# Moving the cross-attention key projection of a fused decoder kernel to an earlier joint, with reciprocal square roots worked partly in PSUM

## The reference

```
x = x + gate * (retention(...) @ ret_w_out)          # first block, layer 0
h = rms_norm(x, norm_g[1]) * (1 + scale) + shift     # first block, layer 1: attention
...
mem_n = rms_norm(mem, norm_mem)                      # (256, 1024), gain norm_mem
x = x + concat(y_a, y_b, y_c) @ w_out                # mixer out
h = rms_norm(x, norm_cross)
q = rms_norm((h @ wq) per head, q_g)                 # 4 heads of 128
kv = mem_n @ wkv
k = rms_norm(kv[..., :512] per head, k_g)
v = kv[..., 512:]
x = x + softmax(q k^T / sqrt(128)) v @ wo
```

## Time and profile before

| what | us |
|---|---|
| device time, three runs | 1804.52, 1806.66, 1806.71 |
| median | 1806.66 |
| the profiled execution, its own time | 1805.74 |
| its span | 1803.9 |
| PE busy | 1763.1 (98%) |
| DVE, ACT, POOL busy | 931.5, 471.5, 1103.0 |
| granted clock of PE, mean | 0.99 |

### The profile page before, as it was taken

How to read it: one execution, slowest core, us unless ns; L and a number is a source line. 1 busy time by engine, 2 the same in 40 slices (tenths; PEclk the granted TensorE clock), 3 DMA queues, 4 the chain that set the end, 5 groups by cost and what they waited for, 6 DMA issues and landing times.

```text
span 1803.9 us, 26195 instructions
## 1 busy us (share of the span) xinstructions
PE 1763.1 (98%) x9198; PEld 1477.0 (82%) x9198; DVE 931.5 (52%) x1534; ACT 471.5 (26%) x958; POOL 1103.0 (61%) x848
## 2 busy tenths in 40 slices
PE   6999999999999999999999999989989999999998
PEld 4888888888888888888888778877878878888887
DVE  4754736574455545555443888786373463213311
ACT  4121221200233222322221247555332422002200
POOL 3656555698455444645457659864066588667863
PEclk9999999999999999999999999999999999999999
DMA  9523222385232222332223322200022333333331
GB/s 359 171 77 94 84 73 76 93 302 166 62 105 81 77 76 77 92 91 76 75 77 104 96 73 59 59 24 25 24 82 76 88 95 103 101 98 88 99 99 54
DMA packets 281588, 172.87 MB, mean 96 GB/s; under 512 B 6000, under 2 KB 272560, under 8 KB 280496
## 3 DMA queue, kind: packets, MB, share of 16 engines
q1 hardware_dynamic: 275024, 151.01, 28.5%
q10 hardware_dynamic: 6496, 20.93, 3.4%
HBM read 169.69 MB, written 2.10 MB: 95 GB/s over the span
## 4 chain that ended last, share of the span: by engine, by line
PE 92%; DVE 6%; SPq 1%; ACT 1%; DMA 0%; issue 0%; DVEq 0%; ACTq 0%
PE acc L390 14%; PE acc L392 14%; PE acc L391 14%; PE ob L390 4%; PE ob L392 4%; PE ob L391 4%; PE acc L420 3%; PE acc L422 3%; PE acc L421 3%; PE sc L1622 2%; PE acc L438 2%; PE acc L439 2%; PE acc L440 2%; PE sc L1543 1%; PE ob L1634 1%; PE acc L2035 1%
## 5 line engine op out<-in xcount | busy, mean ns | idle before, releaser
L766 POOL TENSOR_TENSOR wl<-raw,wh 128x512 fp32r<-128x512 f32 x456 | 638.6, 1421 | 19.3
L763 POOL TENSOR_SCALAR wh<-raw 128x1024 fp32r<-128x1024 f32 (+1 forms) x232 | 268.4, 1157 | 571.2 <-PE acc L392 143.5
L390 PE MATMUL acc<-hh,wh 128*128 128x512 f32 x800 | 325.6, 407 | 1.2 <-ACT sq L1413 1.2
L392 PE MATMUL acc<-hh,wl 128*128 128x512 f32 x800 | 313.7, 392 | 0.0
L391 PE MATMUL acc<-hl,wh 128*128 128x512 f32 x800 | 312.8, 391 | 0.0
L390 PEld LDWEIGHTS acc<-hh,wh 128*128 128x128 f32 x800 | 151.3, 189 | 35.5 <-issue 2.6
L391 PEld LDWEIGHTS acc<-hl,wh 128*128 128x128 f32 x800 | 151.5, 189 | 32.3 <-issue 2.4
L392 PEld LDWEIGHTS acc<-hh,wl 128*128 128x128 f32 x800 | 150.9, 189 | 33.0
L390 PE MATMUL ob<-Yh,wh 128*128 128x512 f32 x256 | 100.5, 393 | 0.0
L392 PE MATMUL ob<-Yh,wl 128*128 128x512 f32 x256 | 99.7, 390 | 0.0
L391 PE MATMUL ob<-Yl,wh 128*128 128x512 f32 x256 | 99.7, 389 | 0.0
(11 more groups left out here) (545 smaller groups left out, 3725.7 us busy)
## 6 DMA issues: line engine op xcount, KB each, us to landing
raw<-in_att_w_in SPq DMA_DIRECT2D x64, 512.0 KB, 4.0
raw<-in_mlp_w SPq DMA_DIRECT2D x64, 512.0 KB, 3.9
raw<-in_ret_w_in SPq DMA_DIRECT2D x48, 512.0 KB, 3.7
ada_w<-in_ada_w ACTq DMA_DIRECT2D x8, 1536.0 KB, 7.0
raw<-in_w_in SPq DMA_DIRECT2D x23, 512.0 KB, 3.6
ada_w<-in_ada_w SPq DMA_DIRECT2D x16, 512.0 KB, 8.9
raw<-in_ret_w_out SPq DMA_DIRECT2D x16, 512.0 KB, 4.3
raw<-in_att_w_out SPq DMA_DIRECT2D x16, 512.0 KB, 4.0
```

The source lines that it names most:

```text
L390: e.matmul(bank[:, :], wh[:, s, k, :], rhs_high(k), start=(start and k == 0), stop=False)
L392: last = e.matmul(bank[:, :], wl[:, s, k, :], rhs_high(k), start=False, stop=(stop and k == k1 - 1))
L763: e.tensor_scalar(wh[:, s, 0:k1, :], raw[:, s, 0:k1, :], 1.0, 1.0, ALU.mult, ALU.mult).then_inc(high_done, 1)
L766: low = e.tensor_tensor(wl[:, s, k0:k0 + KT // 2, :], raw[:, s, k0:k0 + KT // 2, :], wh[:, s, k0:k0 + KT // 2, :].bitcast(F32), ALU.subtract)
```

## The change

UNITS now has xa_k behind ret_out. The memory comes in a second time, transposed by the host (mem_t, 1 MB), so no PE transposes are left. It is loaded twice: into mem_t_early (where hh lies) during ret_out, for the keys, and into mem_t during the mixer's scan, for the values. At the first joint the keys are made without any root into the PSUM banks ob0 and ob1, evicted by ACT into xa_k_early, and written to a DRAM tensor, from which ACT's queue reads them back into xa_k in the second block, where their squares are taken in one ACT instruction and summed on PE behind mix_out unit 5. The token root (two columns) and the key roots (eight) are taken together, behind the mix_out loop. norm_roots and these roots run through roots_bank, which keeps copies in the bank st so that each step has at most one operand in SBUF. DVE's first attention sum waits for the keys' write, since the place is used again.

The diff, cut:

```diff
@@ norm_roots: rsqrt replaced @@
+        def roots_bank(e, a, n, name, work):
+            y, z = rs[:, 0, a:a + n], rs[:, 2, a:a + n]
+            yb, x, zb = (work[:, j, :] for j in range(3))      # in the bank st
+            def both(o, ob_, op):
+                op(ob_).then_inc(*V.done())
+                step(e, op(o), V)
+            both(y, yb, lambda o: e.tensor_scalar(o.bitcast(I32), x.bitcast(I32), -0.5, RSQRT_MAGIC, ALU.mult, ALU.add))
+            step(e, e.tensor_tensor(z, y, yb, ALU.mult), V)
...
         def norm_roots(e, tag, n=S):
             e.wait_ge(*PE.at(f"{tag}cols{KT - 1}"))
-            rsqrt(e, n // P, 1.0 / D, f"{tag}root")
+            w = root_work(n // P)
+            step(e, e.tensor_scalar(w[:, 1, :], st[:, 0:n // P], 1.0 / D, EPS, ALU.mult, ALU.add), V)
+            roots_bank(e, 0, n // P, f"{tag}root", w)
@@ ACT, retention out and first joint @@
             load_ada1(0)
             load_ada1(1)
+            e.dma_start(mte[:, :, :], mem_t).then_inc(mem_t_in, 16)
             ret_out_square(0)
             load_ada1(2)
             ret_out_square(1)
             load_ada1(3)
+            e.wait_ge(mem_t_in, 16)
             for n in range(2, KT):
                 if n % 2 == 0 and n + 3 < KT:
                     load_ada1(n + 2)
                     load_ada1(n + 3)
+                if n < 6:
+                    early_memory(2 * n - 4)
+                    early_memory(2 * n - 3)
+                if n == 6:
+                    early_high(0)
+                    early_high(1)
                 ret_out_square(n)
+            early_keys(0)
             norm_highs(e, "n1", lambda k: mod[:, 1, 0, k:k + 1])
+            early_keys(1)
+            e.wait_ge(*AC.at("x_ke1"))
+            e.dma_start(keys, xke[:, :, :].rearrange("p h n -> p (h n)")).then_inc(keys_out, 16)
@@ PE, first joint @@
+            early_keys(0)
             e.wait_ge(*V.at("mod1"))
             e.wait_ge(*V.at(f"ret_outss{KT - 2}"))
             columns(e, dg, 0, "first", False)
             e.wait_ge(*AC.at(f"ret_outsq{KT - 1}"))
             columns(e, sq[:, 1, :], 0, False, "last", f"n1cols{KT - 1}")
+            early_keys(1)
+            norm_spread(e, "n1")
+            early_keys(2)
             for n in range(16, 24):
                 last = e.matmul(sc[0][:, n:n + 1], ada_acc1[:, n * P:(n + 1) * P], ones[:, 0:1], start=True, stop=True)
             last.then_inc(*PE.done("ada1gate"))
-            norm_spread(e, "n1")
+            early_keys(3)
@@ DVE, retention out; first attention turn @@
                 ret_out_add(n)
+                if n == KT - 2:
+                    early_low(0)
                 ret_out_sum(n)
                 if n == KT - 2:
+                    early_low(1)
...
+            e.wait_ge(keys_out, 16)
             for n in range(4):
                 att_sum(0, "p", n)
@@ PE, second joint @@
-            def memory_steps(j):
-                if j < 2:
-                    memory_turned(2 * j + 4)
-                    memory_turned(2 * j + 5)
-            out_flat("mix_out", V.at(f"g_lo{GH - 1}"), KT, memory_steps)
-            for h in range(XH):          # the 4 xa_k units, with their column sums
...
+            def key_sums(j):
+                if j == 4:
+                    e.wait_ge(*AC.at("x_ksq"))
+                    for h in range(XH):
+                        columns(e, ksq[:, h, :], 16 + 2 * h, True, True, "x_kcols" if h == XH - 1 else None, n=2)
+            out_flat("mix_out", V.at(f"g_lo{GH - 1}"), KT, key_sums)
+            pair(e, U["xa_q"], U["xa_q"], "nx", [V.at(f"mix_outx{KT - 2 + b}") for b in range(2)])
@@ ACT, mix_out loop @@
-                if 1 <= j <= 2:
-                    memory_out(2 * j + 2)
-                    memory_out(2 * j + 3)
+                if 1 <= j <= 4:
+                    memory_out(2 * j - 2)
+                    memory_out(2 * j - 1)
+                if j == 3:
+                    e.wait_ge(keys_in, 16)
+                    e.activation(ksq[:, :, :], xk[:, :, :], ACT.Square).then_inc(*AC.done("x_ksq"))
                     memory_high(0)
@@ DVE, mix_out loop @@
                 mix_out_sum(j)
-                if j == 1:
-                    e.wait_ge(*AC.at("nkss1"))
-                    step(...); step(...)
-                    roots(e, 32, 2, "nkroot")
-                if j == 2:
-                    memory_low(0)
-                if j == 4:
-                    memory_low(1)
-            e.wait_ge(*PE.at("x_cols7"))
+            e.wait_ge(*PE.at("x_kcols"))
+            e.wait_ge(*AC.at("nkss1"))
+            w = root_work(10)
...
+            roots_bank(e, 16, 10, "xk_root", w)
+            memory_low(0)
+            memory_low(1)
```

125 lines of the change are left out of this document (66 added, 59 removed).

## The result

| | kernel before | changed kernel | ratio, 95% interval |
|---|---|---|---|
| first comparison, median | 1806.68 (1804.52 to 1807.44) | 1790.59 (1789.12 to 1792.87) | 0.9916 [0.9904, 0.9928] |
| again, on the chip of the last experiments | 1806.38 (1802.59 to 1808.66) | 1790.48 (1789.56 to 1792.47) | 0.9914 [0.9901, 0.9928] |
| the profiled execution, its own time | 1805.74 | 1789.37 | |
| its span | 1803.9 | 1787.6 | |
| mean granted clock of its span | 0.99 | 0.995 | |

The changed kernel is faster by 16 us in the medians. The forecast was 1795.6 with a range from 1793.0 to 1800.0, so the direction was right and the time came out 5.0 us under the forecast and 2.4 us under the range.

A forecast was written before the change was run, and what follows sets the result against it. PE, busy 98% of the span, was taken to bound the kernel. First joint 4.8 us more and second 15.9 less make 11.1 us less, so the median goes from 1806.66 to 1795.6, range 1793.0 to 1800.0.

The forecast's parts named there:

- First joint: From the last ret_out matmul to the attention's first pair issued: grows by 4.8 us, to 27.3, for 11.5 us of key work.
- one of the marks: Sign that the forecast is right: PE's granted clock is 1.00 between ret_out and the attention.
- The split of the 11.1 us into causes: Keys 1.2, mix_out's transposes and waits 4.3, first joint's clock about 2 and idle time 5, less 1.1 for new bubbles and waits.
- The root: Norm root in the first joint: twelve steps, none with two SBUF operands, 2.4 to 3.0 us; PE waits at most 0.2.
- hl beside POOL, and ACT's queue: First joint: each hl 1.42 us instead of 0.74 beside POOL; ACT's late query eviction costs up to 2.4, taken as 0.2.
- the first rival: First joint's cover incomplete: query eviction 2.4 us, roots 0.8, lower clock 2; time 1798.5 to 1801; chance 0.16.
- the second (clock): Clock stays at half through the whole first joint, key matmuls 8.9 us more: 1806.5, no change; chance 0.07.
- the third (memory late): Slow memory load delays the modulation's sums, PE waits ahead of the last ret_out unit; slower kernel; chance 0.03.
- Ahead of the first joint: Added ACT and DVE work and a 1 MB load before the joint lie in idle time: cost taken as nothing.
- Second joint: From mix_out unit 1 done to the end of the xa_q pair: 43.3 us instead of 59.20, 15.9 less.
- The 2.2 us: PE's wait for a late xT in mix_out, put down to the token root ahead of x2 on DVE, goes away.
- The sum outside the joints: Total of 4.8 minus 15.9, 11.1 us less, which counts no change of time outside the two joints.

The follow-up runs named there:

- the run with fillers: Kernel before, its first joint filled with 96 idle matmuls of 256 columns that no one reads, keys left where they were: 1808.56 us, ratio 1.0017.
- the run with the old roots: Changed kernel with every root taken as before, all operands in SBUF: 1796.36 us, ratio to the kernel before 0.9951.
- the run with the token root back: Changed kernel with the memory's token root taken once more behind tile 1 of mix_out on DVE, result unused: 1799.99 us.

## Why the prediction was right or wrong

- **First joint, 4.8 us more: right, 4.2 in this pair of traces.** The terms were 11.5 and 0.3 for keys and bubbles (11.74 measured), 1.8 for sums (1.70), 0.5 for the spread (0.36), 1.9 for the modulation's columns (1.70), 11.1 and 0.2 for pair and wait (11.25). The small groups are each 0.1 to 0.2 too high; for the modulation's I took the duration of the records (1.93) for their pace, and the next group starts before the last one ends. The clock stayed at 1.00, as one of the marks asked, and the run with fillers shows that this comes from the cover, not from what is computed. The kernel before had a quick draw of this joint, though: over its three traces with the old roots the mean is 23.05 us, and the joint grows by 3.7.
- **The split of the 11.1 us into causes was not right.** It names 5 us of idle time in the first joint, where the earlier trace rows have 22.54 less 18.77, 3.8, and its parts add up to 11.4. The forecast does not hang on it, since it goes by the two joints.
- **The root: the form right, its price too high.** I had 2.4 to 3.0 us from a row of the MLP with a 0.16 us gap behind a PSUM write; it took 2.06. Starts are 0.2 us apart in either form, and twins that write PSUM and SBUF are 0.08 apart. What I did not work out was the old form beside the splits: 7.1 us, 5.8 us of the time. The 0.97 us step that I set beside the rule for two SBUF inputs reads one operand, so it does not bear that rule out; steps that read two were slow in the run with the old roots (1.14 and 1.20 us at 450.06 and 451.24).
- **hl beside POOL, and ACT's queue: right.** 0.9 to 1.4 us each instead of 1.42 throughout; the query's eviction cost 0.2 of the 2.4 that the first rival held against it. That rival did not come, nor the second (clock) nor the third (memory late).
- **Ahead of the first joint: right, nothing.** The last ret_out matmul is 0.07 us later.
- **Second joint, 15.9 us less: right, 16.2.** The 2.2 us were right as a sum over PE's path (43.3 against 42.97). As a cause the token root is larger than the wait it made: removed from the kernel before it gives 2.5 us of path (3.3 in the mean), put back into the changed one it costs 6.4 us of wait and 9.5 us in all.
- **The sum outside the joints: this step failed.** I let everything outside the two joints stand, and the lower end of the range had only the 0.3 us of the change's own terms and the 2.2 us between the runs of before. By the rows the two joints give 4.2 less 16.2, 12.0 us. The profiled times differ by 16.4: the three stretches of code that is the same took 5.1 us less, and the end 0.7 more. Of the 5.1, the 1.6 behind the pair divide every trace of the old second joint from every trace of the changed one, so the term that the sum put at nothing was most likely in part an effect of the change. The other 3.5 lie in half-clock stretches that differ between two executions of one program, of which the trace of before had slow draws. The range had no term for either.
- **The means.** Over all runs shown beside the experiments and here, the kernel before has a mean of 1805.6 us (50 runs) and a mean granted clock of 0.9909, the changed one 1790.8 (9 runs) and 0.9947. That is 14.8 us, give or take 1. The means of the traces add up to it: first joint 3.7 more, from mix_out's first matmul behind the wait for Ml to the end of the pair 16.1 less (65.4 and 49.3), behind the pair 1.6 less, the first two stretches 0.7 and 0.1 less. That it fits to the tenth is luck, with three to nine traces a side. The clock says about the same: 0.0038 of 1800 us is 6.8 us, of which the first joint held 22.54 times 0.23, 5.2, and the stretch behind the pair about the rest, 1.7 (10.64 times 0.16).
- **Where the 4.8 us between the forecast (1795.6) and the mean (1790.8) lie.** The median of three runs that I started from is 1.0 above the mean of the 50. The terms of the two joints were 0.9 short. The other 2.8 are what the sum left out: 1.6 behind the pair, 0.8 in the first two stretches, and 0.4 in the joints, whose single traces were not the mean. Why the stretch behind the pair goes with the second joint stays open, and so does whether the 0.8 are the change or chance.

## What to carry to other kernels

Put independent dense matmuls where a dependent chain leaves PE idle: here 11.5 us of them cost about 4, because they took the place of 4 us of waits and brought back the clock. Then look at what the moved work sets going beside that chain, since a chain of tiny steps with all operands in SBUF became three times as long next to GpSimd's splits, and keeping copies in PSUM saved 5.8 us of the move's gain; parts that measure as nothing or 4 us alone were worth 6 and 9 together. Before a sum is built on a single trace, list its half-clock stretches, in code that stays too, and give the range a term for them; a second trace of the same program tells which of them are drawn anew.

## What the runs showed of the hardware

- Steps of 2 to 10 elements with all operands in SBUF took 0.16 or 0.17 us while POOL was idle (also with PE busy beside them, in the run with fillers), and beside its splits many took 0.7 to 1.2 us (six of nine in the joint with the old roots, six of ten in the run with the token root back). With one operand in PSUM none of twelve was over 0.17 us beside the same splits.
- The granted clock of PE went to its lower level at different places in two executions of one program (0.63 or 1.00 in the same four microseconds). In the stretch from conv_sq to dsa_k_scale the traces lie near 68 or 70 us, for one program too (68.40 and 70.09). Behind the xa_q pair they lie at 9.04 or 10.65, and there no program that was traced twice changed.
- A wait of 4.2 us of PE was followed by a clock of 0.61 over the next 3.2 us and one of 6.4 us by matmuls at 0.43 us; the waits cost 1.7 us each beyond their length. The same wait of 2.2 us had 1.00 behind it in one trace and 0.57 in another.
